# Normalised tokens made beside the first pairs of tiles of a feed-forward, and 256-column products from the tenth pair on

## The reference, cut to what matters

```python
def modulate(h, shift, scale):
    return h * (1 + scale) + shift

def rmsnorm_2(x, g):
    xf = x.astype(jnp.float32)
    y = xf * lax.rsqrt(jnp.mean(xf * xf, axis=-1, keepdims=True) + RMS_EPS)
    return (y * g.astype(jnp.float32)).astype(x.dtype)

def swiglu_2(h, w1, w3, w2):
    return (jax.nn.silu(h @ w1) * (h @ w3)) @ w2

        h2 = modulate(rmsnorm_2(x, norm2_g[i]), sh2, sc2)
        x = x + g2 * swiglu_2(h2, ffn_w1[i], ffn_w3[i], ffn_w2[i])
```

## Time and profile before

| | us |
|---|---|
| median of 3 runs | 995.0 (994.06 to 995.28) |
| the profiled execution's own time | 993.76 |
| its span, first to last instruction | 992.0 |
| PE busy | 977.8 (99%) |
| DVE busy | 789.8 (80%) |
| ACT busy | 556.4 (56%) |
| granted TensorE clock, mean | 0.998 |
| third feed-forward, its first pair's root to its last output tile | about 806 to 983 in the span |

### The profile page before, as it was taken

How to read it: one execution, slowest core, us unless ns; L and a number is a source line. 1 busy time by engine, 2 the same in 40 slices (tenths; PEclk the granted TensorE clock), 3 DMA queues, 4 the chain that set the end, 5 groups by cost and what they waited for, 6 DMA issues and landing times.

```text
span 992.0 us, 19483 instructions
## 1 busy us (share of the span) xinstructions
PE 977.8 (99%) x7774; PEld 945.4 (95%) x7774; DVE 789.8 (80%) x1421; ACT 556.4 (56%) x922; POOL 23.0 (2%) x28
## 2 busy tenths in 40 slices
PE   9999999999999999999999999999999999999997
PEld 6999999999889999999999998899999999999997
DVE  5888889975899979998887778688899787666553
ACT  5654443444877755555544537796755574454442
POOL 4000000000000000000000000000002000000000
PEclk9999999999999999999999999999999999999999
DMA  8667667893443347986678504352626555565541
GB/s 307 213 213 234 213 210 245 286 340 119 139 149 117 98 128 282 321 293 209 223 263 283 195 22 142 119 171 96 244 86 205 178 195 188 185 190 166 173 140 43
DMA packets 53780, 189.05 MB, mean 191 GB/s; under 512 B 6136, under 2 KB 7705, under 8 KB 53050
## 3 DMA queue, kind: packets, MB, share of 16 engines
q1 hardware_dynamic: 53514, 187.21, 56.5%
q10 hardware_dynamic: 176, 0.59, 0.2%
HBM read 186.73 MB, written 1.05 MB: 189 GB/s over the span
## 4 chain that ended last, share of the span: by engine, by line
PE 78%; DVE 14%; ACT 4%; issue 2%; DMA 0%; DVEq 0%; POOL 0%; ACTq 0%; POOLq 0%
PE psum L455 78%; DVE memr L1023 5%; DVE memr L1045 3%; DVE memr L1230 1%; DVE mem L1227 1%; ACT memr L1724 1%; DVE mem L1221 1%; ACT mem L1735 1%; ACT mem L2042 1%; ACT memr L1735 1%; DMA mem<-in_w_up 0%; ACT mem L1866 0%; PE psum L470 0%; DVE psum L1212 0%; DVE mem L1420 0%
## 5 line engine op out<-in xcount | busy, mean ns | idle before, releaser
L455 PE MATMUL psum<-memr 128*128 128x256 f32 (+5 forms) x7534 | 946.5, 288 | 3.8 <-DVE memr L1045 2.1
L455 PEld LDWEIGHTS psum<-memr 128*128 128x128 f32 (+1 forms) x7534 | 918.5, 188 | 25.3 <-issue 7.9
L1023 DVE TENSOR_TENSOR memr<-mem,memr 128x1024 fp32r<-128x1024 f32 (+1 forms) x290 | 339.1, 1207 | 44.0 <-ACT memr L1724 43.7
L1724 ACT ACTIVATE memr<-mem 128x1024 fp32r<-128x1024 f32 (+2 forms) x296 | 290.7, 1026 | 15.1 <-DMA mem<-in_w_down 7.7
L1735 ACT ACTIVATE memr<-mem 128x256 fp32r<-128x256 f32 (+6 forms) x172 | 82.9, 493 | 269.8 <-DVE mem L1155 102.1
L1045 DVE TENSOR_TENSOR memr<-mem,memr 128x256 fp32r<-128x256 f32 (+4 forms) x128 | 58.4, 466 | 10.5 <-ACT memr L1735 9.6
L1140 DVE TENSOR_TENSOR mem<-psum,mem 128x256 f32<-128x256 f32 (+1 forms) x66 | 28.0, 425 | 42.6 <-PE psum L455 42.6
L1732 ACT ACTIVATE mem<-mem 128x256 f32<-128x256 f32 (+1 forms) x56 | 22.9, 415 | 64.9 <-DVE mem L1691 32.4
L1033 DVE CUSTOM_DVE_ANT_0 mem<-mem 128x1024 f32<-128x1024 f32 x48 | 58.6, 1222 | 0.6
L1045 DVE TENSOR_TENSOR memr<-psum,memr 128x256 fp32r<-128x256 f32 (+2 forms) x68 | 31.3, 480 | 7.4 <-ACT memr L1735 6.6
L1811 ACT ACTIVATE mem<-mem 128x256 f32<-128x256 f32 (+1 forms) x66 | 29.9, 453 | 7.0 <-DVE mem L1133 6.0
(11 more groups left out here) (137 smaller groups left out, 379.3 us busy)
## 6 DMA issues: line engine op xcount, KB each, us to landing
mem<-in_w_gate SPq DMA_DIRECT2D x66, 512.0 KB, 4.2
mem<-in_w_up SPq DMA_DIRECT2D x66, 512.0 KB, 4.6
mem<-in_w_ada SPq DMA_DIRECT2D x48, 512.0 KB, 4.5
mem<-in_w_down SPq DMA_DIRECT2D x48, 448.0 KB, 4.3
mem<-in_w_in SPq DMA_DIRECT2D x36, 512.0 KB, 5.0
mem<-in_w_down SPq DMA_DIRECT2D x24, 512.0 KB, 4.6
mem<-in_sb_qkv SPq DMA_DIRECT2D x24, 512.0 KB, 4.6
mem<-in_sb_o SPq DMA_DIRECT2D x8, 512.0 KB, 3.3
```

Source lines behind the costliest of these rows:

```text
L455: return pe.matmul(out, a, b, start=start, stop=stop)
L1023: dve.tensor_tensor(r(ol, n), raw(e), rf(oh, n), ALU.subtract).then_inc(w_lo, 1)
L1724: act.activation(r(oh, n), raw(e), ACT.Copy).then_inc(w_hi, 1)
```

## The change

It concerns the third feed-forward alone. In pairs 1 to 8, behind that pair's own work, DVE and ACT make one feature tile each of normalised and shifted tokens, split in halves, in new areas `NH` and `NL` (8 tiles of 256 columns each; `NU` is a buffer of two for the step between). The new function `normed` has the two DVE steps, and the end of ACT's loop the step between them. From pair 10 on (`NORMED` = 10, twelve pairs, 24 tiles, 576 matmuls) the products take these 256 columns instead of the 258. PE waits once, ahead of pair 10, until all 8 tiles are there (`x2_lo`). In these pairs nothing has to be scaled or shifted any more: ACT takes the Silu straight out of PSUM, and DVE multiplies the up result in PSUM by it, so L1133, L1135, L1140 and L1142 fall away and a plain multiplication takes the place of L1153.

```diff
--- before.py
+++ after.py
@@ -267,6 +267,9 @@
     HH, HL = zip(*[(fa[i].take(NF * FN[i]), fa[i].take(NF * FN[i])) for i in range(3)])
     FTMP = [[[fa[i].take(FN[i]) for _ in range(4)] for _ in range(2)] for i in range(3)]
     FCOL = [fa[2].take(2) for _ in range(2)]
+    NH, NL, NU = fa[2].take(KT * T1), fa[2].take(KT * T1), [fa[2].take(T1) for _ in range(2)]
+
+    NORMED = 10
 
 
     sb = Area(SCR, FFN_LIMIT)
@@ -538,14 +541,17 @@
 
 
         def gate_up(i, m, s=None, order=range(KT)):
-            d, n = W_FFN[i] + 2 * m, FNA[i]
-            pairs = (("g", d, gate_ev), ("u", d + 1, up_ev))
+            normed = i == 2 and m >= NORMED
+            d, n = W_FFN[i] + 2 * m, T1 if normed else FNA[i]
+            pairs = (("g", d, silu_done if normed else gate_ev), ("u", d + 1, prod_done if normed else up_ev))
+            if normed and m == NORMED:
+                pe.wait_ge(x2_lo, 2 * KT)
 
             def xh(kt):
-                return a_hi(kt, 0, n)
+                return r(NH + T1 * kt, T1) if normed else a_hi(kt, 0, n)
 
             def xl(kt):
-                return a_lo(kt, 0, n)
+                return r(NL + T1 * kt, T1) if normed else a_lo(kt, 0, n)
 
             if s is None:
                 for key, t, ev in pairs:
@@ -1114,6 +1120,15 @@
         def ffn(i, root, after, hook=None):
             n, base, shift = FN[i], W_FFN[i], i == 2
 
+            def normed(j):
+                u = f(NU[j % 2], T1)
+                if j > 1:
+                    dve.wait_ge(x2_lo, KT + j - 1)
+                dve.scalar_tensor_tensor(u, hx(j, NMETA, T1), f(G2N + j, 1), f(RSTD, T1), ALU.mult, ALU.mult).then_inc(x2_u, 1)
+                dve.wait_ge(x2_hi, KT + j + 1)
+                dve.scalar_tensor_tensor(r(NL + T1 * j, T1), u, f(MOD + 24 + j, 1), rf(NH + T1 * j, T1),
+                                         ALU.add, ALU.subtract).then_inc(x2_lo, 1)
+
             def finish(m):
                 dve.wait_ge(hid_hi, NF * i + m + 1)
                 minus(r(HL[i] + m * n, n), f(FTMP[i][m % 2][3], n), rf(HH[i] + m * n, n)).then_inc(hid_lo, 1)
@@ -1127,6 +1142,15 @@
                     dve.wait_ge(root_done, root)
                     dve.reciprocal(f(RSTD, n), f(SROOT, n)).then_inc(rstd_done, 1)
                     dve.wait_ge(rstd_done, root)
+                if shift and m >= NORMED:
+                    finish(m - 1)
+                    if m < NF - 1:
+                        low_halves(base + 2 * (m + 1) + 6)
+                    dve.wait_ge(*freed[base + 2 * m + 1])
+                    dve.wait_ge(silu_done, c)
+                    dve.wait_ge(hid_lo, c - 2)
+                    dve.tensor_tensor(f(GG, n), pb(bu, n), f(SSL, n), ALU.mult).then_inc(prod_done, 1)
+                    continue
                 dve.wait_ge(*freed[base + 2 * m])
                 if m >= 2:
                     dve.wait_ge(silu_done, c - 2)
@@ -1156,6 +1180,8 @@
                 last.then_inc(prod_done, 1)
                 if hook:
                     hook(m)
+                if shift and 0 < m <= KT:
+                    normed(m - 1)
             finish(NF - 1)
             low_halves(base + 2 * NF + 6)
             for m in range(KT):
@@ -1805,16 +1831,25 @@
                 if i == 0 and m == 2:
                     act.wait_ge(c_in, 16)
                     act.activation(f(SILC, 2048), f(SILC, 2048), ACT.Silu).then_inc(silc_done, 1)
-                act.wait_ge(gate_ev, c)
-                if m >= 2:
+                if shift and m >= NORMED:
+                    act.wait_ge(*freed[base + 2 * m])
                     act.wait_ge(prod_done, c - 2)
-                act.activation(f(SSL, n), f(TT, n), ACT.Silu, bias=f(FCOL[k], 1) if shift else 0.0).then_inc(silu_done, 1)
+                    act.activation(f(SSL, n), pb(bank_of["g", i, m], n), ACT.Silu).then_inc(silu_done, 1)
+                else:
+                    act.wait_ge(gate_ev, c)
+                    if m >= 2:
+                        act.wait_ge(prod_done, c - 2)
+                    act.activation(f(SSL, n), f(TT, n), ACT.Silu, bias=f(FCOL[k], 1) if shift else 0.0).then_inc(silu_done, 1)
                 if 0 < m < NF - 1:
                     high_halves(base + 2 * (m + 1) + 6)
                 act.wait_ge(prod_done, c)
                 copy(r(HH[i] + m * n, n), f(GG, n)).then_inc(hid_hi, 1)
                 if hook:
                     hook(m)
+                if shift and 0 < m <= KT:
+                    act.wait_ge(x2_u, KT + m)
+                    act.activation(r(NH + T1 * (m - 1), T1), f(NU[(m - 1) % 2], T1), ACT.Identity,
+                                   bias=f(MOD + 23 + m, 1)).then_inc(x2_hi, 1)
             high_halves(base + 2 * NF + 6)
             for m in range(KT):
                 d = base + 2 * NF + 3 * m
```

## The result

The changed kernel takes 999.67 us (median of 4 runs, 999.25 to 1000.37), the kernel before 995.14 on the same chip; the ratio is 1.0052, with a 95% interval of 1.0039 to 1.0064. So it is slower by 3.9 to 6.4 us, with 5.2 as the ratio's own value; the plain difference of the two medians is 4.5, inside that interval. The forecast was 998.5, + 3.5.

A forecast was written before the change was run, and what follows sets the result against it. From the output projection through the third feed-forward only PE's matmul pace and any PE wait were taken to count. Terms - 1.76 + 4.04 + 1.2 = + 3.5 us on the median 995.0 gave 998.5 us, range 996.0 to 1000.4.

The forecast's parts named there:

- The wait: PE ahead of pair 10 stands idle for the last new low half: 4.0 us lost, 0 with no falling back.
- The round of 6.12 us: DVE in pairs 2 to 8: 4.67 us at its best plus 1.45 of new steps, against 5.75 of PE.
- The count by idle time: DVE between product and next L1133: 1.45 us more is less than the idle 1.86, so it fits.
- the ring: Per pair, DVE's low halves wait for ACT's high halves, these for Silu, Silu for DVE's L1133 and L1135: 4.67 us.
- The clock: PE behind its idle time ahead of pair 10: the granted clock falls to half, costing 1.2 us, at most 1.8.
- The two thirds of the first stretch: PE's restart ahead of pair 10: 1.2 us taken, two thirds of the 1.8 us seen at the program's start.
- The columns: Pairs 10 to 21: 576 matmuls of 256 columns in place of 258 save 3.05 ns each, 1.76 us.
- the lower end of my bound, 0.8: Pairs 10 to 21: smallest gain if the new areas are faster, 576 x 1.3 ns = 0.8 us.
- DVE's and ACT's savings from pair 10 on: DVE drops about 1.1 us a pair, ACT reads PSUM; all lies beside the matmuls, worth 0.
- The sum: Whole kernel: - 1.76 + 4.04 + 1.2 = + 3.5 us, 998.5 on the median of 995.0; chance 0.42.
- Slower by more than 0.2%: Whole kernel: measured time above the limit of 997.0 us, chance 0.72; no change had 0.22.

The follow-up runs named there:

- steps and wait alone: Eight new steps and PE's wait ahead of pair 10 added to the kernel before, all 22 pairs on the old 258 columns: 1000.36 us, ratio 1.0060.

## Why the prediction was right, point by point

- *The wait.* Right in place, cause and size: 4.0 us forecast, 4.13 lost, with PE idle for 3.96. The round of 6.12 us put together from the earlier trace rows is 6.14 to 6.15; the 1.06 us from first to third step is the earlier trace rows again. The count by idle time, 1.45 against 1.86, would have called it hidden; moving one step by two places, with the same work, showed that it was the ring.
- *The clock.* Right in kind: the clock falls in the wait and PE restarts at half clock. 1.2 us forecast, 1.46 lost in the change's trace, 1.4 shown by the version with matmuls in the wait, but 2.6 and 2.5 lost in two other traces with the same wait (pair 10's end 6.7 and 6.6 us late, less 4.1 of wait). The two thirds of the first stretch were a guess and came near by luck; they gave no sign that the price takes two values.
- *The columns.* This is the term that was mis-sized: 1.76 us forecast, 0.80 measured. The sentence that failed is "I take 1.76, the value of the same stage, whose operands have the same stride". The same stride gave four paces, by where the operands start. With the start of the output tiles' operands within 256 bytes the stream has their pace and the term is right. The earlier trace rows had shown that equal shapes differ, and the lower end of my bound, 0.8, is what came.
- *The output tiles.* Unforeseen: + 0.59 us, from work that the change doesn't touch.
- *DVE's and ACT's savings from pair 10 on* were worth 0, as forecast: in the traces the matmuls of pairs 12 to 21 follow each other without a gap, and the account closes without such a term.
- *The sum.* + 3.5 forecast, + 5.2 measured by the ratio, + 5.4 in the traces. Terms: wait + 0.1, clock + 0.3, columns + 1.0, output tiles + 0.6 over the forecast. The median, 999.67, lies in the stated range of 996.0 to 1000.4, near its slow end: all four terms erred the same way, so nothing cancelled by luck. Slower by more than 0.2% had 0.72.
- *Two rules of the Trainium skill.* The Trainium skill's formula ("TensorE: Matmul & The Clock Gate", Back-to-back issue gap), which that section calls the gap of an isolated matmul, not that of a stream with a weight load each, makes it 0.8 ns for two columns. On the old areas, the only place run with both counts, dropping them is worth 1.4 ns, between the formula and my 3.05. Its other rule (the Trainium skill, "TensorE: Matmul & The Clock Gate", HAM oscillation) is that idle gaps bring the clock down. The four traces that have the gap of 3.9 us agree, and so does the one in which it is filled.

**What stays open.** The output tiles run at 116.7 or 117.8 ns with the same operands. They had 116.7 in each run whose pairs ended at 116.7 or on the 258 columns, 117.8 behind 117.5 and 120.0 and behind the 256 old columns at 118.3, and behind the new tokens at 118.3 they had either: 116.7 when the stream went over from 258 columns without a stop, 117.8 when it began behind PE's wait. Each of these is one profiled execution, so it isn't shown either that a kernel always has the same value: that the output tiles' pace differs between executions of one kernel was not tested. I can't tell what in PE or in the memory would carry it over, nor why the start within 256 bytes matters. Nor is it settled what makes the half clock last 3.4 or 6.8 us; in the two traces with 3.4 it began 3.6 and 3.7 us behind the end of the last matmul, in the two with 6.8 it began 2.5 and 2.7 behind it. The mean granted clock of each timed execution tells in part how they split. Kernels without the wait have 0.998 or 0.999, that is 1 to 5 us at half clock, so an execution of 0.995 or less (9 us or more at half clock) was at half clock behind the wait for longer than 3.4 us. The version with pair 10 on 258 columns has 0.995 in all four executions, steps and wait alone 0.997, 0.997, 0.995, 0.995 and 0.994, the change 0.998, 0.996, 0.996 and 0.995. But their times don't sort by it (the change's slowest execution, 1000.37 us, is the one at 0.998), so the extra 1.1 us of the long stretch is seen in traces alone.

## What to carry to other kernels

Idle time of an engine is room for more work only if the new work doesn't stand in a ring: find what the engine waits for once it is late (here ACT, which in turn waits for it), count the round in that state, and put a step that waits for another engine behind whatever that engine needs first. Here a wait of 4 us on a saturated TensorE cost its own length and 1.4 to 2.6 us of half clock on top, and 16 matmuls of no use put into it saved the second part. When a buffer for a matmul stream gets a new address, try its start: here, among four offsets within 256 bytes, the same stream took 116.7 to 120.0 ns a matmul, up to 2 us for 576 of them.

## What the runs showed of the hardware

- The pace of a float32r stream of 256 columns, with a new 128 x 128 weight load for each matmul, depends on the moving operands' start: 118.3 ns at the change's place, 120.0 ns 12 words on, 117.5 ns 7 words on, 116.7 ns 60 and 1020 words on.
- The same stream of 528 matmuls ran at 116.7 ns a matmul in nine traces and at 117.8 in five, all along its length. It went with what ran ahead of it, one trace for each version.
- 258 columns took 119.7 ns, 256 columns on the same areas 118.3.
- In 3.9 us without a matmul TensorE's granted clock fell to half (1.2 GHz), 2.5 to 3.7 us behind the last matmul's end, and stayed there for 3.4 us (two traces) or 6.8 us (two traces); with 16 matmuls of 512 columns in that gap it stayed at 2.4 GHz.
